# Modulation sums in four column groups turned by VectorE, first rows shared by two blocks, squares added up on VectorE

## What is computed

```
rms_norm(x, g)  = x * rsqrt(mean(x * x, axis=-1) + 1e-6) * g
h = h + mix;      h = h + conv_ffn(rms_norm(h, ffn_norm))
mod             = silu(c) @ ada_w + ada_b          # per modulated layer, 6 x 1024 columns
y               = rms_norm(x, norm) * (1 + scale) + shift   # scale, shift, gates are slices of mod
```

## Time and profile before

| | us |
|---|---|
| median of 3 runs | 2891.96 (2889.69 to 2896.49) |
| the profiled execution's own time | 2890.2 |
| its span, first to last instruction | 2888.4 |
| TensorE matmuls (PE) busy | 2773.1 |
| VectorE (DVE) busy | 1728.3 |
| ScalarE (ACT) busy | 1028.3 |
| mean granted clock of TensorE | 0.985 |

### The profile page before, as it was taken

One profiled execution on the slowest core, in us unless ns is written; L12 is line 12 of the kernel. 1 busy time (PEld: TensorE's weight loads), 2 busy tenths in 40 slices (PEclk: granted clock), 3 DMA queues, 4 the chain that ended last, 5 costly groups with the idle time before them and its releaser, 6 DMA issues.

```text
span 2888.4 us, 35842 instructions
## 1 busy us (share of the span) xinstructions
PE 2773.1 (96%) x14656; PEld 2250.6 (78%) x14656; DVE 1728.3 (60%) x2488; ACT 1028.3 (36%) x1495; POOL 90.1 (3%) x156
## 2 busy tenths in 40 slices
PE   7999799999998999999999999999999999999998
PEld 6778688888875588888776688888888787888886
DVE  4287657475668557575556647564665888553443
ACT  3244434242333534242434633232332222432322
POOL 0000000000001300000001400000000000000000
PEclk9999999999999999999999999999999999999999
DMA  6711024443232124343321025454432110333221
GB/s 162 158 44 44 30 89 149 126 143 108 73 97 81 30 85 153 124 141 111 88 82 44 1 65 193 159 178 138 143 100 70 34 33 26 107 104 100 88 92 41
DMA packets 261803, 276.85 MB, mean 96 GB/s; under 512 B 23496, under 2 KB 230856, under 8 KB 261641
## 3 DMA queue, kind: packets, MB, share of 16 engines
q1 hardware_dynamic: 231448, 219.51, 25.0%
q10 hardware_dynamic: 30192, 55.05, 5.9%
HBM read 267.19 MB, written 7.34 MB: 95 GB/s over the span
## 4 chain that ended last, share of the span: by engine, by line
PE 86%; DVE 7%; ACT 2%; DMA 2%; issue 1%; SPq 1%; ACTq 0%; POOL 0%; DVEq 0%
PE ps L554 23%; PE ps L556 23%; PE ps L555 23%; PE ps L1154 3%; PE ps L790 2%; PE ps L1186 2%; PE ps L918 1%; DMA sb<-in_hgrn_w_in 1%; PE ps L1113 1%; PE ps L935 1%; PE ps L612 1%; DVE sb L1826 1%; PE ps L1132 1%; DVE sb L2192 1%; PE ps L952 1%
## 5 line engine op out<-in xcount | busy, mean ns | idle before, releaser
L554 PE MATMUL ps<-sb 128*128 128x512 f32 (+2 forms) x3448 | 1286.7, 373 | 31.6 <-ACT sb L1388 5.5
L556 PE MATMUL ps<-sb 128*128 128x512 f32 (+2 forms) x3448 | 1268.0, 368 | 0.0
L555 PE MATMUL ps<-sb 128*128 128x512 f32 (+2 forms) x3448 | 1267.9, 368 | 0.0
L554 PEld LDWEIGHTS ps<-sb 128*128 128x128 f32 x3448 | 651.2, 189 | 162.0 <-issue 36.0
L556 PEld LDWEIGHTS ps<-sb 128*128 128x128 f32 x3448 | 650.7, 189 | 112.4
L555 PEld LDWEIGHTS ps<-sb 128*128 128x128 f32 x3448 | 651.3, 189 | 108.9 <-issue 1.2
L1826 DVE TENSOR_TENSOR sb<-sb 128x2048 fp32r<-128x2048 f32 (+2 forms) x196 | 438.4, 2237 | 357.8 <-ACT sb L1287 357.8
L1287 ACT ACTIVATE sb<-sb 128x2048 fp32r<-128x2048 f32 (+2 forms) x196 | 365.0, 1862 | 286.1 <-PE ps L556 266.7
L2062 DVE SCALAR_TENSOR_TENSOR sb<-ps,sb 128x511 f32<-128x511 f32 (+1 forms) x264 | 197.5, 748 | 172.2 <-ACT sb L1511 166.7
L1511 ACT ACTIVATE sb<-ps,sb 128x512 f32<-128x512 f32 x132 | 99.7, 772 | 233.7 <-PE ps L556 233.6
L2082 DVE SCALAR_TENSOR_TENSOR sb<-sb 128x512 f32<-128x512 f32 x168 | 126.0, 750 | 12.9 <-DVE sb L2082 0.5
(11 more groups left out here) (226 smaller groups left out, 2170.8 us busy)
## 6 DMA issues: line engine op xcount, KB each, us to landing
sb<-in_ffn_w_up SPq DMA_DIRECT2D x88, 1024.0 KB, 5.1
sb<-in_ada_w ACTq DMA_DIRECT2D x192, 256.0 KB, 3.2
sb<-in_ffn_w_down SPq DMA_DIRECT2D x32, 1024.0 KB, 5.0
sb<-in_ffn_w_down SPq DMA_DIRECT2D x16, 768.0 KB, 4.4
sb<-in_hy_w_in SPq DMA_DIRECT2D x12, 1024.0 KB, 5.1
sb<-in_hgrn_w_in SPq DMA_DIRECT2D x8, 1024.0 KB, 11.5
sb<-in_hgrn_w_in SPq DMA_DIRECT2D x16, 512.0 KB, 5.5
sb<-in_dsa_w_in SPq DMA_DIRECT2D x6, 1024.0 KB, 5.2
```

The costliest lines, as they stand in the source:

```text
L554: pe.matmul(o, al, bh, start=f, stop=False, **kw)
L555: pe.matmul(o, ah, bl, start=False, stop=False, **kw)
L556: m = pe.matmul(o, ah, bh, start=False, stop=l, **kw)
```

## The change

Three edits. (1) `ada_finish` sums a block with four matmuls whose stationary operand is 32 columns of ones and whose moving operand is every fourth run of 32 columns of `acc`; each writes its own 32 partitions of bank 6, 128 columns. VectorE turns this with its 32 by 32 transposition (`ada_end`) and adds `ada_b` for the block's four columns at once. Before the sum of block b TensorE waits until block b - 1 has been turned. VectorE turns block b - 2 just before it begins block b, and the last two in the last residual, behind its block 2. (2) `halved_start` takes both blocks side by side on the first half of the tokens: tile k is used by both before tile k + 1. The second half is as before. (3) ScalarE squares tile 0 into the second buffer, tiles 1 to 5 each into the first; VectorE adds each of these onto the second (`accumulate`), one step behind its additions onto x, and number 5 behind the low half of the weights. TensorE sums the total once, where it summed squares 4 and 5.

```diff
--- before.py
+++ after.py
@@ -527,6 +527,11 @@
+        def ada_sums(n, b):
+            c = 128 if b == ADA[n][2] - 1 else 0
+            return ps[6][:, c:c + 128]
         def scale_of(n):
@@ -650,8 +655,7 @@
                     if j == 0:
-                        squared(4)
-                        squared(5)
+                        squared(None)
                 for j in range(2):
@@ -667,30 +671,35 @@
                 stage, i = NEXT[r]
-                for half in range(2):
-                    ready = lambda k: [("h", stage, half, k, "hi"), ("h", stage, half, k, "lo")]
+                ready = lambda half, k: [("h", stage, half, k, "hi"), ("h", stage, half, k, "lo")]
+                for n in range(2):
+                    for b in banks[n]:
+                        wait_bank(b)
+                for k in range(NT):
                     for n in range(2):
-                        if half == 0:
-                            for b in banks[n]:
-                                wait_bank(b)
-                        for k in range(NT):
-                            for j in range(2):
-                                m = project_half(keys[n], j, half, banks[n][j], (k,), ready)
-                                if half and k == NT - 1:
-                                    m.then_inc(*mark(sem, done[n][j], *([("used", keys[n])] if j else [])))
-                                    freed[banks[n][j]] = then[n][j]
-                            if half == 0 and n == 0 and k == 2:
-                                squared_half(r, 1)
-                        if half == 0 and n == 0:
-                            spread_half(stage, i, 1)
+                        for j in range(2):
+                            project_half(keys[n], j, 0, banks[n][j], (k,), lambda k: ready(0, k))
+                    if k == 2:
+                        squared_half(r, 1)
+                    elif k == 5:
+                        spread_half(stage, i, 1)
+                for n in range(2):
+                    for k in range(NT):
+                        for j in range(2):
+                            m = project_half(keys[n], j, 1, banks[n][j], (k,), lambda k: ready(1, k))
+                            if k == NT - 1:
+                                m.then_inc(*mark(sem, done[n][j], *([("used", keys[n])] if j else [])))
+                                freed[banks[n][j]] = then[n][j]
             def residual(sem, r, keys, banks, ready, tile=None, stats=True, gain=False, amid=None, late=None):
                 def squared(j):
                     for i in ((0, 1) if gain else (0,)):
-                        if j == 0:
+                        if j is None:
                             wait_bank((STAT, OTHER)[i])
-                        pe.wait_ge(*at("sq", r, i, j))
-                        sums((STAT, OTHER)[i], (ht if i else sq)[j % 2], j == 0, j == NT - 1).then_inc(
+                            pe.wait_ge(*at("acc", r, i, 5))
+                        else:
+                            pe.wait_ge(*at("sq", r, i, j))
+                        sums((STAT, OTHER)[i], (ht if i else sq)[1 if j in (None, 7) else 0], j is None, j == NT - 1).then_inc(
                             *mark("pe_stat", ("sq_used", r, i, j), *([("stat", r, i)] if j == NT - 1 else [])))
@@ -706,14 +715,10 @@
                         project(sem, keys[n], banks[n % 2], names, then, tile=tile, ready=ready, cols=(0,))
-                        squared(4)
-                        squared(5)
+                        squared(None)
                         project(sem, keys[n], banks[n % 2], names, then, tile=tile, ready=ready, cols=(1,))
...
                         project(sem, keys[n], banks[n % 2], names, then, tile=tile, ready=ready)
-                        if stats and n:
-                            squared(2 * n - 2)
-                            squared(2 * n - 1)
                 if stats and r not in NEXT:
@@ -851,13 +856,17 @@
+                    blocks = ADA[n][2]
                     for b in range(done[0], upto):
-                        wait_bank(6)
+                        if b == 0:
+                            wait_bank(6)
+                        elif b < blocks - 1:
+                            pe.wait_ge(*at("ada_turned", n, b - 1))
                         pe.wait_ge(*at("ada", n, 8 * b + 7))
-                        for i in range(4):
-                            c = 4 * b + i
-                            m = pe.matmul(ps[6][:, c:c + 1], acc[b % 2][:, 128 * i:128 * i + 128], ones[:, 0:1], start=True, stop=True,
-                                          skip_group_check=True)
+                        own = acc[b % 2].rearrange("p (c g i) -> p g c i", g=4, i=32)
+                        for g in range(4):
+                            m = pe.matmul(ada_sums(n, b)[32 * g:32 * g + 32, :].rearrange("p (c i) -> p c i", i=32), ones[:, 0:32], own[:, g],
+                                          start=True, stop=True, skip_group_check=True)
                         m.then_inc(*mark("pe_ada", ("ada_sum", n, b)))
@@ -879,7 +888,7 @@
                     ada_finish(ADA[n][2])
-                    freed[6] = [("mod", n)]
+                    freed[6] = [("ada_turned", n, ADA[n][2] - 1)]
@@ -1337,7 +1346,7 @@
                 act.wait_ge(*at("x", r, j, half))
-                act.wait_ge(*at("sq_used", r, 0, j - 2))
+                act.wait_ge(*(at("acc", r, 0, 5) if j == 6 else at("sq_used", r, 0, None)))
                 act.activation(sq[j % 2][:, hs], x[:, j, hs], ACTF.Square).then_inc(*mark("act_sq", ("sq", r, 0, j, half)))
@@ -1346,9 +1355,11 @@
                     act.wait_ge(*at("x", r, j))
-                    dst = (ht if i else sq)[j % 2]
-                    if j >= 2:
-                        act.wait_ge(*at("sq_used", r, i, j - 2))
+                    dst = (ht if i else sq)[1 if j in (0, 7) else 0]
+                    if j == 7:
+                        act.wait_ge(*at("sq_used", r, i, None))
+                    elif j >= 2:
+                        act.wait_ge(*at("acc", r, i, j - 1))
                     act.activation(dst[:, :], x[:, j, :], ACTF.Square, scale=g).then_inc(*mark("act_sq", ("sq", r, i, j)))
@@ -1913,14 +1924,23 @@
                 stage, base = NEXT[r][0], 48 * layer + 8 * first
-                dve.wait_ge(*at("mod", 2 if layer else 1))
+                dve.wait_ge(*at("mod", 2 if layer else 1, ADA[2 if layer else 1][2] - 1))
                 dve.tensor_scalar(g1c[:, :], mod[:, base + 8:base + 16], 1.0, None, ADD).then_inc(*step("g1", stage, 0))
...
-            def residual(r, banks, keys, scale=None, stats=True):
+            def accumulate(r, j, gain):
+                for i in ((0, 1) if gain else (0,)):
+                    one, total = ht if i else sq
+                    dve.wait_ge(*at("sq", r, i, j))
+                    if j > 1:
+                        dve.wait_ge(*at("acc", r, i, j - 1))
+                    dve.tensor_tensor(total[:, :], total[:, :], one[:, :], ADD).then_inc(*mark("dve_acc", ("acc", r, i, j)))
+            def residual(r, banks, keys, scale=None, stats=True, gain=False, late=None):
                 ended[r] = banks, scale
@@ -1936,8 +1956,14 @@
                         m.then_inc(*mark("dve_x", ("x", r, j)))
+                        if stats and 2 <= j < 6:
+                            accumulate(r, j - 1, gain)
                     if n < 3 or not stats:
                         ahead(keys[n])
+                    if stats and n == 2:
+                        accumulate(r, 5, gain)
+                    if late and n == 2:
+                        late()
@@ -2064,6 +2090,20 @@
+                def ada_end(b):
+                    layer, b0, blocks = ADA[n]
+                    c0, t = 48 * layer + 4 * (b0 + b), acc[b % 2][:, 0:128]
+                    dve.wait_ge(*at("ada_sum", n, max(b, blocks - 1) if b >= blocks - 2 else b))
+                    dve.transpose(t, ada_sums(n, b)).then_inc(*mark("dve_ada", ("ada_turned", n, b)))
+                    dve.wait_ge(*at("ada_turned", n, b))
+                    dve.tensor_tensor(mod[:, c0:c0 + 4], t.rearrange("p (c i) -> p c i", i=32)[:, :, 0], v("ada_b", c0, 4), ADD).then_inc(
+                        *mark("dve_ada", ("mod", n, b)))
+                def ada_rest():
+                    for b in range(ADA[n][2] - 2, ADA[n][2]):
+                        ada_end(b)
                 def ada(slot):
@@ -2074,7 +2114,8 @@
                             if b >= 2:
-                                dve.wait_ge(*at("ada_sum", n, b - 2))
+                                ada_end(b - 2)
+                                dve.wait_ge(*at("mod", n, b - 2))
                             dve.wait_ge(*at("cact"))
@@ -2114,13 +2155,8 @@
                 gi = len(GROUPS) - 1
-                residual(r0 + gi, ((0, 1), (4, 5)), [(stage, "down", gi, j) for j in range(4)], scale)
-                if n in ADA:
-                    layer, b0, blocks = ADA[n]
```

(8 more changed lines are left out.)

## The result

Before 2893.07 us (median of 4, 2889.69 to 2896.49), after **2929.7 us** (median of 4, 2925.71 to 2936.14): the ratio is 1.0129, 95% interval 1.0106 to 1.0151. Slower, as forecast, but by 36.6 us where the sum said 21.8, and outside the range 2897 to 2923. The profiled execution took 2929.14 us against 2890.2, span 2927.3 against 2888.4: +38.9.

What follows compares the result with a forecast made beforehand. TensorE, busy 96% of the span, was taken as the bound. The terms -15.2 + 35.2 + 12 - 13.8 - 8.4 + 12 gave +21.8 us on 2890.2, so 2912 us, range 2897 to 2923.

Steps and rivals of the forecast that it cites:

- A: Residuals: fewer visits of sums of squares on TensorE save 15.2 us.
- B: End of seven residuals: TensorE waits 4.9 to 5.4 us each for accumulate 5 on VectorE, +35.2 us.
- C: Behind the seven new waits TensorE's clock falls, 1.7 us each, +12 us, bounds 0 and 14.7.
- D: First rows of six stages: sharing tiles between two blocks removes 2.3 us of tile waits each, -13.8 us.
- E: 24 modulation blocks: a sum in column groups costs 0.55 us instead of 0.90, -8.4 us.
- F: Block 1 of three ffn stages: TensorE waits for turned modulation blocks, 3.4, 3.4 and 5.2 us, +12 us.
- fourth rival: Shared first rows change nothing because VectorE's tiles set the pace: D near 0, F smaller, 2919 us; chance 3%.
- first rival: Waits come as in B, but the clock does not fall behind them: 2900 us; chance 18%.
- ffn waits: Rival: every turned block is late, not only block 1, some 8 more waits, 12 us together, 2924 us; chance 9%.
- rival of a hidden wait: Accumulate 5 arrives within the half block, so B and C vanish: -25.4 us, 2865 us; chance 8%.

Runs made afterwards that it cites:

- run 6: Kernel before with one edit alone, VectorE's and TensorE's order mended: added squares 2879.81 us, ratio 0.9955; modulation sums, turned mid-block, 2882.8 us, 0.9964.
- run 3: Changed kernel plus 26 unneeded matmuls before the wait for accumulate 5 in seven residuals: 2914.62 us, ratio 1.0072 to the kernel before.
- run 4: Kernel before with only the shared first rows (halved_start) added: 2891.72 us, ratio 1.0004.
- Run 1: Changed kernel with accumulate 5 moved ahead of the low half of the next weights on VectorE: 2886.8 us, ratio 0.9985 to the kernel before.
- run 2: Changed kernel with each edit undone alone: squares in pairs again 2895.3 us, shared first rows undone 2923.23 us, modulation sums by columns again 2921.66 us.
- kernel with late banks: Changed kernel with both waits mended and block 1 joining the shared first rows only from tile 3, after catching up: 2875.27 us, ratio 0.9946.

## Why the prediction was wrong

| term | predicted | measured | where |
|---|---|---|---|
| A fewer sums | -15.2 | -11.4 (-16.5 to -9.3) | run 6 |
| B wait for the added squares | +35.2 | +33.2 | waits after |
| C clock | +12 | +26.8, of which 17.0 at the seven waits | windows, run 3 |
| D shared rows | -13.8 | +0.5 (-1.4 to +3.5 as a time) | run 4 |
| E modulation sums | -8.4 | -8.45 | run 6 |
| F wait for turned blocks | +12 | +6.8, and 1.7 of clock, counted in C | waits after |

The measured terms sum to 47.5 where the spans differ by 38.9. They come from different kernels, and the medians of A and E hold those kernels' own losses to the clock, which row C counts for the changed kernel alone. With the clock taken out of A and E (-19.5 and -11.5) the sum is 36.3; the rest isn't explained. Against the prediction C was off by +14.8 us, D by +14.3, A by +3.8, F by -5.2 and B by -2.0. The total was off by 14.8 by the medians, so some errors took each other away.

**B was right** in place, mechanism and size, though 2.0 us too large: 4.74 to 5.04 us in six residuals. In residual 8 it is 3.91 instead of 5.4. Run 1 shows the cause that part B named (both halves in front of accumulate 5). Residual 17 has no wait, as forecast.

**D is the step that failed.** It said that two blocks at a time would take 2.3 us of tile waits away in each of six stages, -13.8 us; run 4 shows +0.5. "8.5 us of work, 2.5 of waits for tiles" took the waits as a remainder of prices; the trace had them as rows, 0.61 and 0.77, and the missing 1.1 was never a wait in these rows. It then took the banks of block 1 as free. In the order before, block 1 is begun late, so VectorE's second half of x7 cost nobody anything; moving block 1 to the head put its bank behind VectorE's tiles 0 and 1 (1.17 to 2.42 us in six stages, 9.5 in all). And it didn't ask who waits behind the stage: the gate convolution's bank leaves 0.6 us in ffn0. The bounds -15 to -6 did not hold 0, though the fourth rival did, at 3%.

**C was undersized**, by as much as D was wrong. The mechanism held at seven of seven places, and the first rival (the clock holds) is out. The 1.7 us was the mean of three stretches of 6 us that began behind the wait; three places cost that, four 2.9 to 3.1, so a bound of 7 x 2.1 was too low. The kernel before already had a dearer case: behind its longest wait (11.9 us, L1021, at 903 us) the clock cost 2.4 us, and the prediction left it out. Some 10 us more than before were lost elsewhere: 1.7 behind a wait of part F, 1.7 at the start of hy, directly behind the wait of 2.42 us for a bank that part D brought, 3.4 in hgrn at places that no edit touches (the last section shows what stands in front of them), and the remainder, as a balance, in longer falls at places that had one before. TensorE: Matmul & The Clock Gate in the Trainium skill, HAM oscillation, says that each repeated wait brings a fall, for waits of about 3 to 5 us; the seven waits of 3.9 to 5.0 us here agree. Behind the six of 0.7 to 1.0 us in run 1's profiled execution no fall followed directly.

**E was right.** By rows a visit fell from 0.90 to 0.55 us, as the prediction took it, which is 8.4 us for 24; that run 6's medians differ by 8.45 is closer than their interval (-14 to -7) can vouch for. The full saving by columns alone (-16.3) didn't come, so the fixed part of a visit is real; that TensorEngine Tiling (Array Packing) of the Trainium skill, Key Properties, names the change of tiling mode as a drain fits this, and no run here separates it from other fixed costs. The transposition takes 0.309 us (24 of them, 7.4 us), 0.3 was taken. **F** came at block 1 of each of the three stages, as named, with 1.8, 1.8 and 3.2 us instead of 3.4, 3.4 and 5.2 (515.2 - 511.9 is 3.3 by the prediction's own numbers): TensorE did not have D's lead of 2.3 us. Without that lead the prediction's numbers give 1.1, 1.1 and 2.9, and with edit 2 undone (run 2) the waits are 1.4, 1.4 and 2.9. So a part of D's error and F's took each other away: together they were off by 9.1 us, D alone by 14.3.

The other rivals: blocks after block 1 brought no waits, so the ffn waits did not grow; of the shared rows that change nothing (3%) the cause came true, but not its 2919. The rival of a hidden wait (8%, faster) did not happen, but its ground was sound: VectorE had the room. It needed the addition in the right place, and run 1 gave it.

## What to carry to other kernels

When work goes from the busiest engine to an idle one, look at what stands in front of it in the idle engine's own order: one 2.3 us instruction ahead of the result cost 33 us of waits and 15 to 17 us of clock, and moving it cost nothing. Read waits from their rows and not as the remainder of a sum of prices, and for any block that is begun earlier ask who still reads its banks. A saving at the head of a stage ends at the next bank that another engine frees.

## What the runs showed of the hardware

Filling seven waits of 4 to 5 us with idle matmuls made the kernel 15 us faster, since the clock stayed at its upper level.

Short waits matter too, but not each time: the three waits for turned blocks (1.4 to 3.2 us), in six kernels that have them, were followed by a fall in 10 of 18 cases, 1.5 to 3.1 us each.

In hgrn, between 187 and 327 us, where no edit reaches, some executions show a series of falls. The kernel with late banks had four there, 27 us apart; the kernel before had one, at 319 us. TensorE is busy while the clock is low, but each fall stands directly behind a pair of short waits of TensorE, 1.1 us for VectorE and 0.77 us for ScalarE. The same pair in both kernels, with the 4 us behind it, first with late banks, then before:

```profile
243.24 1.10 PE L791 MATMUL ps<-sb 128*128 128x256 f32 x4 [1.10 <-DVE sb L2014]
...
245.11 1.49 PE L812 MATMUL ps<-sb 128*128 128x256 f32 x3 [0.77 <-ACT sb L1462]
245.00:249.00 4.00, 3.89 (x17) 3.56 (x17) 3.25 (x5) 0.00 (x0) 0.00 (x0) 0.57 0.00 0
```

```profile
240.87 1.10 PE L782 MATMUL ps<-sb 128*128 128x256 f32 x4 [1.10 <-DVE sb L1984]
...
242.74 1.10 PE L803 MATMUL ps<-sb 128*128 128x256 f32 x4 [0.77 <-ACT sb L1447]
243.00:247.00 4.00, 4.00 (x28) 3.63 (x28) 2.90 (x5) 1.78 (x3) 0.00 (x0) 1.00 0.00 0
```

The pair comes six times in this stretch, some 25.5 us apart, in each of the 13 profiled executions. Of these 78 pairs 15 were followed by a fall and 63 by none, and no fall stands there without a pair in front. What decides between them no run here shows. The changed kernel had two such falls in one execution and three in the other. Each costs 1.6 to 1.7 us; the runs of one kernel spread by some 10 us, and a difference of less than that between two profiled spans says little until the clock's loss is taken out of both.
